# Attention scores of a decoder layer in two matmul passes in place of three, with doubled key parts

## The chip, the core and the metric

The kernel runs on one core of one Trainium2 chip. The metric is device time in microseconds (us) of one launch; less is better. The work of the core is shared by TensorE (PE, matmuls; its weight loads are listed apart as PEld), VectorE (DVE), ScalarE (ACT) and SyncE (SP), which here only issues DMAs. GpSimd does almost nothing.

## What is computed

A decoder layer for 512 positions of width 1024: half-step SwiGLU FFN, a mixing stage, and a second FFN, with RMS norms between. The mixing stage has two attentions over one shared projection: a stick-breaking one (8 heads of 64) and a dilated sliding-window one (4 key/value heads of 64, three query groups each). The part around the change, cut from the reference:

```python
z = jnp.einsum('bhqd,bhkd->bhqk', qb, kb).astype(jnp.float32) * scale       # stick-breaking, 8 heads
...
sc = jnp.einsum('bhqd,bhqmd->bhqm', qblk[g], kg).astype(jnp.float32) * scale  # dilated, 3 groups x 4 heads
```

All of it is float32. The kernel gets that precision from TensorE by splitting each operand into a high part (the value rounded to the type `float32r`) and a low part (the rest), and adding three passes: high by high, high by low, low by high.

## The kernel before, in words

**Products.** `product` (lines 1176 to 1179) issues the three passes: line 1177 multiplies the high parts, 1178 takes the low part of the moving operand, 1179 the low part of the stationary one. Every projection "unit" (128 output columns over all 1024 inputs, `unit`, line 1206) is 8 such products of 128x512, so 24 matmuls; "Ua" and "Ub" are its first and second half.

**Order of the mixing stage.** `mix_schedule` (line 106) writes out one list of steps, and all engines walk through it in that order. There are 22 attention units (`MIX_ORDER`: q and k and v of four stick-breaking head pairs, and rq, rk, rv of two dilated pairs), then 8 gate units. Half units are used as filling between the attention steps: `scores` h is the score matmuls of stick-breaking head h, `suffix` h and `pv` h its later matmuls, `dscores` (j, r) the scores of dilated head j and residue r (16 of them), `dturn` transposes their probabilities and `dpv` multiplies them with the values.

**Query and key parts.** A unit of q or k holds a pair of heads: head 0 in rows 0 to 63, head 1 in rows 64 to 127. Step `fin` splits it: ACT copies the whole 128x512 tile into the high part (line 666, tiles `sq_hi`, `sk_hi`, `dq_hi`, `dk_hi`), DVE subtracts to make the low part (line 1029 or 1045). The rotary units (rq, rk) are first put together from four 32-row copies on ACT (line 632) and three DVE operations (971, 1035, 1040).

**Score matmuls.** Head a of a pair uses rows 64a to 64a+63 of all four tiles, so each pass works on 64 rows. Stick-breaking: four key blocks with 384 and 128 columns (bank 0), 256 (bank 1) and 512 (bank 2), three passes each, and a bf16 mask matmul of 128 rows for each block (line 1364). Dilated: three groups with 512, 128 and 128 columns, three passes each, then two mask matmuls (lines 1408 and 1409). Lines 1349 and 1398 make PE wait until the low parts of the pair exist.

**Weights.** SP loads one 512 KB unit of weights at a time into a ring of four (`load`, line 417, DMA at line 423). The load of unit u waits until DVE has made the low part of unit u-4 (`w_lo`, line 762), because that frees the ring slot.

## Time and profile before

| | us |
|---|---|
| median of 3 runs (1153.1 to 1154.5) | 1153.97 |
| the profiled execution's own time | 1153.61 |
| its span, first to last instruction | 1151.8 |
| PE busy | 1113.0 (97%) |
| DVE busy | 774.1 (67%) |
| ACT busy | 543.4 (47%) |
| mean granted TensorE clock, 1 is 2.4 GHz | 0.982 |

How to read it: a matmul's start is when its first column goes in; matmuls overlap, so what a matmul costs is the distance from its start to the start of the next one, not its own duration. In the chain of work that ended last PE has 84%, DVE 9%, ACT 4%. The mixing stage runs from about 375 to 660 us.

### The profile page before, as it was taken

How to read it: one execution, taken by the hardware profiler on the slowest of the kernel's cores; microseconds unless marked ns; L12 is line 12 of the kernel's file. 1: busy time of each engine (PE TensorE's matmuls, PEld its weight loads, DVE VectorE, ACT ScalarE, POOL GpSimd, SP SyncE). 2: the span in 40 equal slices, each digit the busy share in tenths (PEclk: the TensorE clock that was granted, in tenths of full speed). 3: DMA queues.
4: the chain of work that ended last, by engine and by line, in shares of the span. 5: the costliest groups of instructions: out<-in, count | busy, mean ns of one | idle time of the engine just before them, and what ended most of it. 6: DMA issues, size and time to landing. Idle time of an engine off the chain costs nothing.

```text
span 1151.8 us, 15666 instructions
## 1 busy us (share of the span) xinstructions
PE 1113.0 (97%) x6058; PEld 953.9 (83%) x6066; DVE 774.1 (67%) x1085; ACT 543.4 (47%) x874; POOL 0.2 (0%) x4
## 2 busy tenths in 40 slices
PE   7799999999999999998899999999899999999996
PEld 6689899988998788887677788888798899989985
DVE  6866378845878778677575555666785478637854
ACT  6544155523653456666555433323553256424641
POOL 0000000000000000000000000000000000000000
PEclk9999999999999999998899999999999999999998
DMA  8133233332324212111020123433233232333221
GB/s 283 56 110 92 92 111 107 98 108 92 99 72 123 84 44 66 46 55 41 33 73 28 38 87 94 140 105 95 74 104 99 92 111 96 98 100 110 80 68 74
DMA packets 32904, 102.99 MB, mean 89 GB/s; under 512 B 4160, under 2 KB 5568, under 8 KB 32832
## 3 DMA queue, kind: packets, MB, share of 16 engines
q1 hardware_dynamic: 32832, 102.01, 28.1%
q8 instruction: 47, 0.77, 0.3%
q14 instruction: 25, 0.20, 0.1%
HBM read 99.90 MB, written 2.10 MB: 89 GB/s over the span
## 4 chain that ended last, share of the span: by engine, by line
PE 84%; DVE 9%; ACT 4%; issue 3%; DMA 0%; DVEq 0%; SPq 0%; ACTq 0%
PE acc_pair L1177 24%; PE acc_pair L1179 23%; PE acc_pair L1178 23%; PE pair_bank L1177 2%; PE pair_bank L1178 2%; PE pair_bank L1179 2%; DVE w_lo L762 2%; PE bank L1177 1%; PE bank L1179 1%; PE bank L1178 1%; ACT w_hi L474 1%; ACT rope L632 1%; DVE t_lo L815 1%; PE bank L1185 1%; DVE rstd L787 1%
## 5 line engine op out<-in xcount | busy, mean ns | idle before, releaser
L1177 PE MATMUL acc_pair<-xg_hi,w_hi 128*128 128x512 f32 (+1 forms) x684 | 265.7, 388 | 7.2 <-DVE w_lo L992 7.2
L1178 PE MATMUL acc_pair<-xg_lo,w_hi 128*128 128x512 f32 (+1 forms) x684 | 259.8, 380 | 0.0
L1179 PE MATMUL acc_pair<-xg_hi,w_lo 128*128 128x512 f32 (+1 forms) x684 | 258.6, 378 | 0.0
L474 ACT ACTIVATE w_hi<-w_raw 128x1024 fp32r<-128x1024 f32 (+2 forms) x158 | 152.6, 975 | 152.0 <-PE acc_pair L1179 151.9
L762 DVE TENSOR_TENSOR w_lo<-w_raw,w_hi 128x1024 fp32r<-128x1024 f32 (+2 forms) x158 | 177.5, 1125 | 47.2 <-ACT w_hi L474 46.5
L1177 PEld LDWEIGHTS acc_pair<-xg_hi,w_hi 128*128 128x128 f32 x684 | 131.9, 193 | 29.9 <-issue 8.4
L1179 PEld LDWEIGHTS acc_pair<-xg_hi,w_lo 128*128 128x128 f32 x684 | 131.2, 192 | 25.0
L1178 PEld LDWEIGHTS acc_pair<-xg_lo,w_hi 128*128 128x128 f32 x684 | 132.1, 193 | 20.2 <-issue 0.7
L1179 PE MATMUL acc_pair<-hid_hi,w_lo 128*128 128x512 f32 x352 | 138.8, 394 | 0.0
L1178 PE MATMUL acc_pair<-hid_lo,w_hi 128*128 128x512 f32 x352 | 138.2, 393 | 0.0
L1177 PE MATMUL acc_pair<-hid_hi,w_hi 128*128 128x512 f32 x352 | 136.9, 389 | 0.0
L931 DVE SCALAR_TENSOR_TENSOR x<-acc_pair,x 128x512 f32<-128x512 f32 x56 | 38.7, 692 | 114.0 <-PE acc_pair L1179 113.8
L1178 PEld LDWEIGHTS acc_pair<-hid_lo,w_hi 128*128 128x128 f32 x352 | 66.1, 188 | 15.1
L1177 PEld LDWEIGHTS acc_pair<-hid_hi,w_hi 128*128 128x128 f32 x352 | 66.1, 188 | 14.4
L1179 PEld LDWEIGHTS acc_pair<-hid_hi,w_lo 128*128 128x128 f32 x352 | 66.2, 188 | 13.4
L510 ACT ACTIVATE s_hi<-s_raw 128x1536 fp32r<-128x1536 f32 x36 | 53.5, 1487 | 48.2 <-DVE s_raw L835 48.2
L850 DVE TENSOR_TENSOR s_lo<-s_raw,s_hi 128x1536 fp32r<-128x1536 f32 x36 | 63.3, 1759 | 13.9 <-ACT s_hi L510 13.9
L1177 PE MATMUL acc_pair<-t_hi,s_hi 128*128 128x256 f32 x216 | 61.1, 283 | 2.6 <-ACT acc_pair L559 2.6
L862 DVE TENSOR_TENSOR acc_pair<-acc_pair,ysum 128x512 f32<-128x512 f32 x36 | 25.2, 700 | 57.2 <-PE acc_pair L1179 57.2
L1179 PE MATMUL acc_pair<-t_hi,s_lo 128*128 128x256 f32 x216 | 61.1, 283 | 0.0
L1178 PE MATMUL acc_pair<-t_lo,s_hi 128*128 128x256 f32 x216 | 61.0, 282 | 0.0
L525 ACT ACTIVATE gate<-gate 128x512 f32<-128x512 f32 x44 | 27.5, 626 | 48.1 <-DVE gate L864 48.1
(217 smaller groups left out, 2092.8 us busy)
## 6 DMA issues: line engine op xcount, KB each, us to landing
w_raw<-in_w13b SPq DMA_DIRECT2D x44, 512.0 KB, 3.6
w_raw<-in_w13a SPq DMA_DIRECT2D x40, 512.0 KB, 3.6
w_raw<-in_wmix SPq DMA_DIRECT2D x22, 512.0 KB, 3.5
w_raw<-in_w2a SPq DMA_DIRECT2D x16, 512.0 KB, 3.6
w_raw<-in_w2b SPq DMA_DIRECT2D x16, 512.0 KB, 3.6
w_raw<-in_wgate SPq DMA_DIRECT2D x8, 512.0 KB, 3.5
w_raw<-in_wend SPq DMA_DIRECT2D x8, 512.0 KB, 3.5
w_raw<-in_wo SPq DMA_DIRECT2D x8, 512.0 KB, 3.6
```

Source lines behind the costliest of these rows:

```text
L474: act.activation(w_hi[:, s, 0:width], w_raw[:, s, 0:width], ACT.Copy).then_inc(whi_done, 1)
L510: act.activation(s_hi[:, g % 2], s_raw[:], ACT.Copy).then_inc(s_hi_done, 1)
L525: act.activation(gate[:, f % 2, :], gate[:, f % 2, :], ACT.Silu).then_inc(silu_done, 1)
L632: act.activation(rope2[to:to + HD // 2, t % 2, :].rearrange("c (r p) -> c r p", r=DIL), acc[w % RING][c:c + HD // 2, :].rearrange("c (p r) ...
L762: dve.tensor_tensor(w_lo[:, s, 0:width], w_raw[:, s, 0:width], w_hi[:, s, 0:width].bitcast(F32), ALU.subtract).then_inc(wlo_done, 1)
L787: dve.reciprocal(rstd[:], mean[:]).then_inc(rstd_done, 1)
L850: dve.tensor_tensor(s_lo[:, g % 2], s_raw[:], s_hi[:, g % 2].bitcast(F32), ALU.subtract).then_inc(s_lo_done, 1)
L862: dve.tensor_tensor(late, late, p5, ALU.add).then_inc(p5_added, 1)
L931: dve.scalar_tensor_tensor(x[:, m, :], acc[s][:], scale, x[:, m, :], ALU.mult, ALU.add).then_inc(acc_read[s], 1)
L1177: pe.matmul(o, w_h, r_h, start=first, stop=False, skip_group_check=check)
L1178: pe.matmul(o, w_h, r_l, start=False, stop=False, skip_group_check=check)
L1179: return pe.matmul(o, w_l, r_h, start=False, stop=last, skip_group_check=check)
```

## The change

The tiles of query and key parts are laid out anew. Each head gets its own slot of 128 rows: in `sq2` and `dq2` the high part of the query lies in the head's 64 rows and the low part in the other 64 rows. In `sk2` and `dk2` the high part of the key lies in the head's 64 rows, and a DMA copies it into the other 64 rows (two DMAs of 64x512 float32, 128 KB each, per key unit; six key units). One pass of 128 rows then gives key high by query high plus key high by query low; a second pass of 64 rows gives key low by query high. For this

- each score product is 2 matmuls: one of 128 rows, one of 64 rows (before: 3 of 64 rows);
- ACT makes the high part in two instructions of 64x512 (before: one of 128x512), for each of the 16 q, k, rq and rk units; DVE makes the low part in two as well;
- SP issues the two copies of key unit w right behind the weight load of unit w+7, after a wait for the high parts (`op_hi_done`);
- PE waits for the copies (`twin_done`) ahead of the scores that use them.

The core of the diff (the renaming of buffers, and the counts `split_parts` in other waits, are left out):

```diff
@@ sync engine @@
-            for u in range(MIX, GATE):
-                load(u, 0, A["wmix"][u - MIX])
-            for u in range(GATE, END):
-                load(u, 0, A["wgate"][u - GATE])
+            for u in range(MIX, END):
+                load(u, 0, A["wmix"][u - MIX] if u < GATE else A["wgate"][u - GATE])
+                if u - 7 in KEYS:
+                    sp.wait_ge(op_hi_done, split_parts(u - 7 - MIX + 1))
+                    for head in (0, 1):
+                        key = stacked(u - 7, head)
+                        sp.dma_start(key[head_rows(head + 1), :].bitcast(F32), key[head_rows(head), :].bitcast(F32)).then_inc(twin_done, 16)
@@ scalar engine, fin @@
-                    act.activation(dst, src, ACT.Copy).then_inc(op_hi_done, 1)
+                    if what in ("v", "rv"):
+                        act.activation(dst, src, ACT.Copy).then_inc(op_hi_done, 1)
+                    else:
+                        for head in (0, 1):
+                            rows = head_rows(head)
+                            act.activation(stacked(w, head)[rows, :], src[rows, :], ACT.Copy).then_inc(op_hi_done, 1)
@@ vector engine, fin (q and k; rq and rk alike) @@
-                        dve.wait_ge(op_hi_done, fin)
-                        dve.tensor_tensor(lo[:, pair % 2, :], src, hi[:, pair % 2, :].bitcast(F32),
-                                          ALU.subtract).then_inc(op_lo_done, 1)
+                        dve.wait_ge(op_hi_done, split_parts(fin))
+                        for head in (0, 1):
+                            rows, hi = head_rows(head), stacked(w, head)
+                            lo = hi[head_rows(head + 1), :] if what == "q" else sk_lo[rows, pair % 2, :]
+                            dve.tensor_tensor(lo, src[rows, :], hi[rows, :].bitcast(F32),
+                                              ALU.subtract).then_inc(op_lo_done, 1)
@@ tensor engine, scores @@
-                    pe.wait_ge(op_lo_done, through(("q", hp, 0), ("k", hp, 0)))
+                    pe.wait_ge(op_lo_done, split_parts(through(("q", hp, 0), ("k", hp, 0))))
+                    pe.wait_ge(twin_done, 32 * (KEYS.index(MIX + MIX_ORDER.index(("k", hp, 0))) + 1))
...
-                            product(o, sk_hi[rows, hp % 2, ks], sk_lo[rows, hp % 2, ks],
-                                    sq_hi[rows, hp % 2, P * i:SEQ], sq_lo[rows, hp % 2, P * i:SEQ],
-                                    n == 0, False, True)
+                            pe.matmul(o, sk2[:, hp % 2, a, ks], sq2[:, hp % 2, a, P * i:SEQ], start=n == 0,
+                                      stop=False, skip_group_check=True)
+                            pe.matmul(o, sk_lo[rows, hp % 2, ks], sq2[rows, hp % 2, a, P * i:SEQ], start=False,
+                                      stop=False, skip_group_check=True)
@@ tensor engine, dscores @@
-                    product(bank[0], dq_hi[jp][rows, 0, own], dq_lo[jp][rows, 0, own], dk_hi[jp][rows, :],
-                            dk_lo[jp][rows, :], True, False, True)
-                    for g in (1, 2):
-                        product(bank[1][:, (g - 1) * P:g * P], dq_hi[jp][rows, g, own], dq_lo[jp][rows, g, own],
-                                dk_hi[jp][rows, own], dk_lo[jp][rows, own], g == 1, False, True)
+                    for g in range(NG):
+                        o = bank[1][:, (g - 1) * P:g * P] if g else bank[0]
+                        keys = own if g else slice(0, SEQ)
+                        pe.matmul(o, dq2[jp][:, a, g, own], dk2[jp][:, a, keys], start=g < 2, stop=False,
+                                  skip_group_check=True)
+                        pe.matmul(o, dq2[jp][rows, a, g, own], dk_lo[jp][rows, keys], start=False, stop=False,
+                                  skip_group_check=True)
```

PE, the first scores of the mixing stage (head 0 of the first pair), before. The names are output, moving and stationary operand; the last number is the columns:

```order
L1177 MATMUL pair_bank<-sq_hi,sk_hi 128x384 [waits consts_made,const_loaded,mean_done,op_lo_done]
L1178 MATMUL pair_bank<-sq_lo,sk_hi 128x384
L1179 MATMUL pair_bank<-sq_hi,sk_lo 128x384
L1177 MATMUL pair_bank<-sq_hi,sk_hi 128x128
L1178 MATMUL pair_bank<-sq_lo,sk_hi 128x128
L1179 MATMUL pair_bank<-sq_hi,sk_lo 128x128
L1364 MATMUL pair_bank<-mask_sb,identb 128x128 x2
L1177 MATMUL pair_bank<-sq_hi,sk_hi 128x256
L1178 MATMUL pair_bank<-sq_lo,sk_hi 128x256
L1179 MATMUL pair_bank<-sq_hi,sk_lo 128x256
```

And with the change (`sq` and `sk` are `sq2` and `sk2`):

```order
L1386 MATMUL pair_bank<-sq,sk 128x384 [waits consts_made,mean_done,const_loaded,twin_done,op_lo_done]
L1388 MATMUL pair_bank<-sq,sk_lo 128x384
L1386 MATMUL pair_bank<-sq,sk 128x128
L1388 MATMUL pair_bank<-sq,sk_lo 128x128
L1391 MATMUL pair_bank<-mask_sb,identb 128x128 x2
L1386 MATMUL pair_bank<-sq,sk 128x256
L1388 MATMUL pair_bank<-sq,sk_lo 128x256
L1391 MATMUL pair_bank<-mask_sb,identb 128x128
L1386 MATMUL bank<-sq,sk 128x512
```

Each block has one matmul less, and the wait at the head of the scores has `twin_done` in addition. A matmul of line 1386 works on 128 rows, one of line 1388 on 64.

SP, the loads of the mixing units before, all in one run:

```order
L423 DMA w_raw<-in_w2a 128x768 [waits wlo_done] x4
L423 DMA w_raw<-in_wmix 128x1024 [waits wlo_done] x22
L423 DMA w_raw<-in_wgate 128x1024 [waits wlo_done] x8
```

And with the change:

```order
L438 DMA w_raw<-in_wmix 128x1024 [waits wlo_done] x9
L471 DMA sk<-sk 64x512 [waits op_hi_done]
L471 DMA sk<-sk 64x512
L438 DMA w_raw<-in_wmix 128x1024 [waits wlo_done] x3
L471 DMA sk<-sk 64x512 [waits op_hi_done]
L471 DMA sk<-sk 64x512
L438 DMA w_raw<-in_wmix 128x1024 [waits wlo_done] x2
L471 DMA dk_0<-dk_0 64x512 [waits op_hi_done]
L471 DMA dk_0<-dk_0 64x512
```

The copies of the first key unit (number 1) stand behind nine weight loads, those of the second (number 4) three loads later, and so on; all go through the queue of the loads.

## Rows read from the trace of the kernel before

**Rows 1.** Windows; columns: us, busy PE PEld DVE ACT POOL, clock, DMA share, GB/s
```profile
375.00:521.00 146.00, 145.12 (x720) 117.60 (x718) 108.61 (x176) 87.77 (x149) 0.00 (x0) 0.98 0.18 58
521.00:620.00 99.00, 89.42 (x426) 70.12 (x432) 64.31 (x123) 58.45 (x95) 0.00 (x0) 0.93 0.16 48
```

**Rows 2.** Waits of PE, 375 to 660 us: total us, times, longest
```profile
PE pair_bank L1177 <- ACT prob L713: 3.9, 4, 2.3
PE bank L1418 <- ACT prob L719: 3.9, 4, 1.6
```

**Rows 3.** Timeline of PE, scores of head 1: start us, us, engine, line, operation
```profile
406.54 0.39 PE L1179 MATMUL acc_pair<-xg_hi,w_lo 128*128 128x512 f32 x1
406.86 0.44 PE L1177 MATMUL pair_bank<-sq_hi,sk_hi 64*128 64x384 f32 x1
407.13 0.33 PE L1178 MATMUL pair_bank<-sq_lo,sk_hi 64*128 64x384 f32 x1
407.31 0.33 PE L1179 MATMUL pair_bank<-sq_hi,sk_lo 64*128 64x384 f32 x1
```

**Rows 4.** Timeline of PE, one dilated score block
```profile
645.27 0.49 PE L1177 MATMUL pair_bank<-dk_hi,dq_hi 64*128 64x512 f32 x1
645.61 0.39 PE L1178 MATMUL pair_bank<-dk_lo,dq_hi 64*128 64x512 f32 x1
645.84 0.39 PE L1179 MATMUL pair_bank<-dk_hi,dq_lo 64*128 64x512 f32 x1
...
646.47 0.27 PE L1178 MATMUL pair_bank<-dk_lo,dq_hi 64*128 64x128 f32 x1
646.58 0.27 PE L1179 MATMUL pair_bank<-dk_hi,dq_lo 64*128 64x128 f32 x1
646.79 0.39 PE L1408 MATMUL pair_bank<-mask_g,identb 128*128 128x512 bf16 x1
```

**Rows 5.** Timeline of SP: when the weight loads w+7 of key units w went out
```profile
387.42 0.33 SPq L423 DMA_DIRECT2D w_raw<-in_wmix  x1
416.47 0.33 SPq L423 DMA_DIRECT2D w_raw<-in_wmix  x1
451.74 0.33 SPq L423 DMA_DIRECT2D w_raw<-in_wmix  x1
496.39 0.33 SPq L423 DMA_DIRECT2D w_raw<-in_wmix  x1
```

**Rows 6.** DMA issues: count, KB each, median us from issue to landing
```profile
w_raw<-in_wmix SPq DMA_DIRECT2D x22, 512.0 KB, 3.5
x<-in_xT SPq DMA_DIRECT2D x8, 256.0 KB, 6.8
w_raw<-in_wend SPq DMA_DIRECT2D x8, 256.0 KB, 2.6
w_raw<-in_wend SPq DMA_DIRECT2D x8, 128.0 KB, 2.2
```

**Rows 7.** Timeline of PE: first matmul of scores 0, 2, 4 and 6
```profile
388.04 0.44 PE L1177 MATMUL pair_bank<-sq_hi,sk_hi 64*128 64x384 f32 x1 [0.71 <-DVE sk_lo L1029]
419.57 0.44 PE L1177 MATMUL pair_bank<-sq_hi,sk_hi 64*128 64x384 f32 x1
459.10 0.44 PE L1177 MATMUL pair_bank<-sq_hi,sk_hi 64*128 64x384 f32 x1
499.41 0.44 PE L1177 MATMUL pair_bank<-sq_hi,sk_hi 64*128 64x384 f32 x1
```

**Rows 8.** Groups with shapes: a copy of 64 rows on ACT | busy us, mean ns
```profile
L699 ACT ACTIVATE ys_hi<-ysum 64x512 fp32r<-64x512 f32 x8 | 5.0, 628 | 0.3 <-DVE ysum L1081 0.2
```

**Rows 9.** Timeline around the split of dilated key unit 17
```profile
553.73 0.63 ACT L666 ACTIVATE dk_hi<-roped 128x512 fp32r<-128x512 f32 x1
554.47 0.69 DVE L1045 TENSOR_TENSOR dk_lo<-roped,dk_hi 128x512 fp32r<-128x512 f32 x1 [1.80 <-ACT dk_hi L666]
557.15 0.66 PE L1418 MATMUL bank<-identf,prob 128*128 128x128 f32 x4 [1.55 <-ACT prob L719]
```

**Rows 10.** Window behind the first scores: same columns as rows 1
```profile
390.00:395.00 5.00, 5.00 (x16) 3.71 (x16) 3.53 (x7) 4.84 (x9) 0.00 (x0) 0.66 0.04 16
```

More of the change, by code:

```diff
@@ L177, in through, with split_parts @@
     return max(MIX_ORDER.index(u) for u in units) + 1
+def split_parts(n):
+    return sum(1 if what in ("v", "rv") else 2 for what, _, _ in MIX_ORDER[:n])
+KEYS = [u for u in FINS if mix_kind(u)[0] in ("k", "rk")]
 ROPES = [u for u in FINS if mix_kind(u)[0] in ("rq", "rk")]
@@ L269, in build @@
                 prob = sb("prob", [P, 2, 6 * P], F32, att)
-                dq_hi = [None, None]
-                dq_lo, dk_hi, dk_lo, dv = ([None, None] for _ in range(4))
+                dq2, dk2, dk_lo, dv = ([None, None] for _ in range(4))
                 def dl_buffers(jp, where):
-                    dq_hi[jp] = sb(f"dq_hi{jp}", [P, NG, SEQ], F32R, where)
-                    dq_lo[jp] = sb(f"dq_lo{jp}", [P, NG, SEQ], F32R, where)
-                    dk_hi[jp] = sb(f"dk_hi{jp}", [P, SEQ], F32R, where)
+                    dq2[jp] = sb(f"dq2_{jp}", [P, 2, NG, SEQ], F32R, where)
+                    dk2[jp] = sb(f"dk2_{jp}", [P, 2, SEQ], F32R, where)
                     dk_lo[jp] = sb(f"dk_lo{jp}", [P, SEQ], F32R, where)
@@ L346, in build @@
         op_lo_done = sem("op_lo_done")
+        twin_done = sem("twin_done")
         z_done = sem("z_done")
@@ L381, in head_rows, with stacked @@
             return slice(HD * (h % 2), HD * (h % 2) + HD)
+        def stacked(w, head):
+            what, pair, g = mix_kind(w)
+            if what == "q":
+                return sq2[:, pair % 2, head, :]
+            if what == "k":
+                return sk2[:, pair % 2, head, :]
+            return dq2[pair][:, head, g, :] if what == "rq" else dk2[pair][:, head, :]
         def v_parts(t):
@@ L648, in _ @@
                         act.wait_ge(raw_done, n + 1)
-                        dst = (sq_hi if what == "q" else sk_hi)[:, pair % 2, :]
                         src = raw[:, w % 2, :]
@@ L652, in _ @@
                         act.wait_ge(rope_step, 2 * (ROPES.index(w) + 1))
-                        dst = dq_hi[pair][:, g, :] if what == "rq" else dk_hi[pair][:]
                         src = roped[:]
@@ L1040, in _ @@
                         dve.tensor_tensor(roped[:], src, turn, ALU.add).then_inc(rope_step, 1)
-                        hi = dq_hi[pair][:, g, :] if what == "rq" else dk_hi[pair][:]
-                        lo = dq_lo[pair][:, g, :] if what == "rq" else dk_lo[pair][:]
                         dve.wait_ge(rope_step, 2 * t + 2)
-                        dve.wait_ge(op_hi_done, fin)
-                        dve.tensor_tensor(lo, roped[:], hi.bitcast(F32), ALU.subtract).then_inc(op_lo_done, 1)
+                        dve.wait_ge(op_hi_done, split_parts(fin))
+                        for head in (0, 1):
+                            rows, hi = head_rows(head), stacked(w, head)
+                            lo = hi[head_rows(head + 1), :] if what == "rq" else dk_lo[pair][rows, :]
+                            dve.tensor_tensor(lo, roped[rows, :], hi[rows, :].bitcast(F32),
+                                              ALU.subtract).then_inc(op_lo_done, 1)
                     else:
                         hi, lo = v_parts(sv[:, pair % 2, :, :] if what == "v" else dv[pair][:])
-                        dve.wait_ge(op_hi_done, fin)
+                        dve.wait_ge(op_hi_done, split_parts(fin))
                         dve.tensor_tensor(lo,
@@ L1203, in bank_free @@
                 else:
-                    pe.wait_ge(op_lo_done, last - MIX + 1)
+                    pe.wait_ge(op_lo_done, split_parts(last - MIX + 1))
             def unit(u0, i, rhs, ks, before=None, half=None):
@@ L1382, in _ @@
                     hp = w // 2
-                    pe.wait_ge(op_lo_done, through(("v", hp, 0)))
+                    pe.wait_ge(op_lo_done, split_parts(through(("v", hp, 0))))
                     pe.wait_ge(a_split, 3 * w + 3)
@@ L1421, in _ @@
                     jp = w // 2
-                    pe.wait_ge(op_lo_done, through(("rv", jp, 0)))
+                    pe.wait_ge(op_lo_done, split_parts(through(("rv", jp, 0))))
                     pe.wait_ge(pt_split, DIL * (w + 1))
```

14 lines of the change are left out of this document (7 added, 7 removed).

## Prediction, made before the changed kernel was run

> **What bounds the kernel now.** The windows come first, since the change touches only the mixing stage. From 375 to 521 us PE is busy 145.1 of 146 us at a clock of 0.98; from 521 to 620 us it is busy 89.4 of 99 us at 0.93 [rows 1]. So the first part is bound by the matmuls, and the second (the dilated attention) by turns by the matmuls and by something that PE waits for. The list of waits names it: the probabilities, 3.9 us in four waits of the score matmuls and 3.9 us in four waits of the transposes [rows 2]. Behind both stands one chain: scores on PE, then maximum, exp, sum and scaling on DVE and ACT, then the transposes on PE. Whatever joins that chain on DVE or ACT is paid; whatever leaves PE there is paid back only in part. For the rest I read the timelines instruction by instruction, because the change takes matmuls that are short.
>
> **What the removed pass costs.** One pass of 384 columns takes 0.18 us from start to start [rows 3], one of 512 takes 0.23 and one of 128 takes 0.11 [rows 4]; for 256 columns I take 0.12, between them. A stick-breaking head has one block of each width, so it loses 0.18 + 0.11 + 0.12 + 0.23 = 0.64 us; eight heads lose 5.1 us. A dilated block loses 0.23 + 2 x 0.11 = 0.45 us; sixteen lose 7.2 us. Together 12.3 us, all on PE.
>
> **What the new passes add on PE.** Before, a block went through its passes with 64 rows throughout, and the number of rows changed only at its ends. What such a change costs can be read. Coming from 128 rows, the first score matmul starts 0.32 us after a 512-column pass that otherwise takes 0.23: 0.09 of nothing. It then takes 0.27 us to the next start, where the same pass takes 0.18 afterwards: another 0.09 to 0.11, in which its weights are loaded in the open [rows 3]. The dilated block shows the same, 0.34 against 0.23 for its first pass, and at its end, from 64 rows to 128, 0.21 against 0.11 [rows 4]. So a change of rows costs 0.09 us of drain and 0.11 of open loading, 0.20 in all; where the pass behind it has 128 columns the loading was what it cost before, so the pass goes from 0.11 to 0.25 (drain, load, 0.05 of columns): 0.14 more. The new code alternates 128 and 64 rows. The Trainium skill (TensorEngine Tiling (Array Packing), Key Properties) says that changing the tiling mode drains TensorE; by that rule, which gives no time, the trace agrees, with 0.09 us at each change.
>
> Counted out: a stick-breaking head before had three changes to 64 rows (at its start and behind two masks); now it has four, one per block, and one more back to 128 rows between the two blocks of bank 0. Two changes at 0.20 make +0.40, so a head comes to -0.64 + 0.40 = -0.24 and eight to **-1.9 us**. A dilated block now has a first pass of 0.23, a second of 0.41 (0.09 + 0.11 + 0.21) and four narrow ones of 0.25, then a drain of 0.09: 1.73 us. Before it was 1.52 from its first start to the mask [rows 4] plus the drain ahead, 1.61. That is +0.12 a block, **+1.9 us** for sixteen. On PE alone the change is worth nothing.
>
> **The copies.** They are new, and they are late by construction: those of key unit w leave behind the load of unit w+7, and this load leaves when DVE has the low part of w+3. The loads that matter went out at 387.42, 416.47, 451.74 and 496.39 us [rows 5]; the scores that need these keys began at 388.04, 419.57, 459.10 and 499.41 [rows 7]. A weight load lands 3.5 us after its issue; 128 KB alone lands after 2.2, and from 128 to 512 KB that is 0.43 us for each 128 KB [rows 6]. Do the copies queue behind the load? The same 256 KB take 2.6 us alone and 6.8 in the crowd at the start [rows 6], so transfers of this queue do stand behind each other. I take 3.5 + 2 x 0.43 = 4.4 us from the load's issue; the lower bound is 3.0 (issued 0.4 and 0.7 after the load, each landing as if alone), the upper 5.0. The skill (DMA: Bandwidth & Descriptors, Queues, rings and completion order) says each engine takes the descriptors of a ring in order; by that rule the copies come behind the load's data, and nothing here shows it for copies inside the chip.
>
> - Scores 0: the split halves (below) put the load at 388.0; + 4.4 is 392.4, against 388.04: **+4.4 us** (bounds 3.0 and 5.0). PE has nothing else in its queue: it is in order, and all units behind the scores wait too.
> - Scores 2: 416.5 + 4.4 = 420.9 against 419.6: **+1.4** (0 and 2).
> - Scores 4: 456.1 against 459.1: hidden, 3 us to spare.
> - Scores 6: 496.4 + 0.6 of a longer split + 4.4 = 501.4 against 499.4: **+2.0** (0.5 and 2.7).
> - The dilated keys are copied tens of us ahead: hidden. SP's own waits for the high parts hold the next load back by nothing, since that load waits for a DVE step that comes later in the list.
>
> **The halves.** A 64x512 copy on ACT takes 0.63 us [rows 8], as long as one of 128 rows [rows 9]; the same holds for DVE. Sixteen units so add 16 x 0.60 us to both, and since DVE waits for both halves, a split that lies on the chain grows by 1.2 us. In the stick-breaking part PE is ahead of nothing that this delays, except near 521 us, where DVE has no idle time left behind the last rq unit. In the dilated part the chain runs through the splits: DVE waits 1.80 us for `dk_hi`, makes `dk_lo`, and the transposes wait 1.55 us behind that [rows 9]. Four more splits lie there (rk, and three rq of pair 1). Five splits at 1.2 are 6.0; some 1.0 of it falls into gaps that PE fills with other matmuls: **+5.0 us** (bounds 1.5 and 8).
>
> **The clock.** After the short wait and the thin scores at 388 us the granted clock of a 5 us window is 0.66 [rows 10], so 3.4 us at the lower level (1.2 GHz), worth 1.7 us. A stop of 4.4 us in the same place, and two new ones, make one more such stretch likely: **+1.7** (bounds -1.7 and +5).
>
> **Sum.** 4.4 + 1.4 + 2.0 - 1.9 + 1.9 + 5.0 + 1.7 = +14.5 us. The profiled execution took 1153.61 us, so 1168.1; it lies 0.4 us under the median of the runs, so I say 1168.3. A measurement of this kernel can tell about 0.2% (2.3 us) from no change.
>
> **Rivals.**
> 1. *The drains are not paid* (faster). If the 64-row weights could be loaded under a running 128-row pass, PE gains the full 12.3 us; with halves wholly hidden and copies at the lower bounds (3.0 + 0 + 0.5) the sum is 12.3 - 3.5 = 8.8 less: 1145; with the copies as forecast 1149. The point from which it decides is a change of rows under 0.06 us. Against it: 0.09 and the open load at every change in rows 3 and 4. Chance 5%.
> 2. *The copies overtake the load.* Then they cost 3.0 + 0 + 0.5 in place of 7.8: 1164. For it: 128 KB alone lands in 2.2. Chance 22%.
> 3. *The halves are hidden.* DVE was busy only 64.3 of 99 us in the dilated part [rows 1]; if slack takes most of 5.0 the time is 1164, with rival 2 together 1160. Chance 18%.
> 4. *The chain of DVE and ACT takes over earlier.* DVE and ACT lie close behind PE from 465 us on; then splits of q and rq there count too (+3), and the clock falls at every stop (+3): 1175. Chance 15%.
> 5. *Nothing changes* because gains on PE and waits cancel, near 1154: 2%. That the passes do not go is excluded: PE has 80 matmuls less in the order, 4 for each of eight heads and 3 for each of sixteen blocks.
>
> **How the numbers follow.** The forecast has 38%. The range takes in rivals 2, 3 and 4 and stops short of the ends where all bounds meet: 1158 to 1176. Faster has rival 1 and a little for two favourable bounds together (6%), same 2%, slower the rest (92%).
>
> **What would show it.** PE: starts of a 128-row and the following 64-row score pass 0.09 us further apart than columns need, and each dilated block near 1.7 us. Waits: PE on the copies at scores 0, 2 and 6, about 5, 1.4 and 2 us. DMA issues: 128 KB copies landing about 4 us after issue. Dilated part: PE's waits for the probabilities grown from 7.8 to about 12 us. Wrong, if the first wait is under 2 us, if a block takes under 1.5 us, or if PE's waits for the probabilities stay near 8.

## The result, and the profile after

| | before | changed |
|---|---|---|
| median of the runs | 1154.01 us (1153.1 to 1154.5) | 1176.19 us (1173.58 to 1182.47) |
| ratio to before, 95% interval | | 1.0201, 1.016 to 1.0242 |
| profiled execution, its span | 1153.61, 1151.8 us | 1175.81, 1173.6 us |

The change is slower by 22.2 us, where 14.3 were forecast: the sign was right, and the time lies 0.2 us above the range. From the start to 375 us (PE busy 360.7 us before, 360.9 now) and over the last 491 us (478.1 and 478.2) the two traces differ by nothing that matters; all of it happens in the mixing stage. Its windows, in the columns of [rows 1], with the end of the stage added:

```profile
375.00:521.00 146.00, 133.61 (x597) 104.04 (x595) 103.35 (x164) 82.47 (x138) 0.00 (x0) 0.91 0.21 63
521.00:620.00 99.00, 89.23 (x391) 66.42 (x391) 67.63 (x123) 61.54 (x103) 0.00 (x0) 0.93 0.14 41
620.00:700.00 80.00, 79.02 (x355) 59.96 (x354) 43.56 (x80) 39.36 (x61) 0.00 (x0) 1.00 0.17 49
```

Up to 521 us PE was busy 145.12 us before and is busy 133.61 now, and the clock of that stretch fell from 0.98 to 0.91. The waits of PE, 375 to 725 us, answer to [rows 2]:

```profile
PE pair_bank L1386 <- issue: 10.9, 3, 6.3
PE bank L1449 <- ACT prob L740: 5.4, 3, 2.9
PE pair_bank L1435 <- ACT prob L734: 3.8, 4, 2.1
PE bank L1210 <- DVE dq L1069: 1.6, 1, 1.6
PE bank L1210 <- issue: 1.5, 2, 1.0
```

The first line is the wait of the scores for the copied rows: its releaser is called "issue" because the profile ties no engine to it, and a DMA had to land. The two waits for the probabilities grew only from 7.8 to 9.2 us. The first scores, and the copies that they wait for, against [rows 5] and [rows 7]:

```profile
388.60 0.33 SPq L438 DMA_DIRECT2D w_raw<-in_wmix  x1
388.97 1.17 SPq L471 DMA_DIRECT2D sk<-sk  x2
...
393.87 0.66 PE L1386 MATMUL pair_bank<-sq,sk 128*128 128x384 f32 x1 [6.28 <-issue]
```

The load went out 1.2 us later than before, and PE could go on 5.3 us after it. By the DMA issues a copy lands after 4.2 us (median) where it stands behind a load, and after 2.3 for the dilated keys:

```profile
sk<-sk SPq DMA_DIRECT2D x8, 128.0 KB, 4.2
...
dk<-dk SPq DMA_DIRECT2D x4, 128.0 KB, 2.3
```

The clock behind that stop and behind two later ones (windows of 5 us, columns as in [rows 10]):

```profile
390.00:395.00 5.00, 1.13 (x2) 0.57 (x2) 0.88 (x2) 0.00 (x0) 0.00 (x0) 0.64 0.48 143
395.00:400.00 5.00, 5.00 (x15) 3.08 (x15) 1.67 (x3) 3.54 (x8) 0.00 (x0) 0.50 0.00 0
400.00:405.00 5.00, 5.00 (x22) 4.06 (x21) 4.71 (x9) 3.66 (x5) 0.00 (x0) 0.84 0.00 0
430.00:435.00 5.00, 5.00 (x14) 2.85 (x14) 0.69 (x1) 3.39 (x7) 0.00 (x0) 0.50 0.00 2
580.00:585.00 5.00, 5.00 (x14) 3.70 (x14) 2.70 (x7) 1.71 (x3) 0.00 (x0) 0.50 0.32 105
```

At 0.50 (1.2 GHz) PE is busy all the time, and a projection pass of 512 columns starts every 0.43 us in place of every 0.23. The same place cost before one window of 0.66 [rows 10]. But a stretch at the lower clock also comes without a stop. The kernel before has windows of 0.82 and 0.84 from 480 to 490 us, and between 390 and 510 us its PE stands still nowhere for more than 0.15 us at a time. Its window from 485 us:

```profile
485.00:490.00 5.00, 5.00 (x20) 4.00 (x20) 3.12 (x6) 4.29 (x9) 0.00 (x0) 0.84 0.00 0
```

A dilated block and the scores of head 1, which answer to [rows 4] and [rows 3]:

```profile
645.35 0.39 PE L1435 MATMUL pair_bank<-dk,dq 128*128 128x512 f32 x1
645.67 0.50 PE L1437 MATMUL pair_bank<-dk_lo,dq 64*128 64x512 f32 x1
646.10 0.33 PE L1435 MATMUL pair_bank<-dk,dq 128*128 128x128 f32 x1
646.35 0.32 PE L1437 MATMUL pair_bank<-dk_lo,dq 64*128 64x128 f32 x1
646.60 0.33 PE L1435 MATMUL pair_bank<-dk,dq 128*128 128x128 f32 x1
646.86 0.32 PE L1437 MATMUL pair_bank<-dk_lo,dq 64*128 64x128 f32 x1
647.12 0.39 PE L1439 MATMUL pair_bank<-mask_g,identb 128*128 128x512 bf16 x1
```

```profile
414.24 0.33 PE L1386 MATMUL pair_bank<-sq,sk 128*128 128x384 f32 x1
414.50 0.44 PE L1388 MATMUL pair_bank<-sq,sk_lo 64*128 64x384 f32 x1
414.87 0.33 PE L1386 MATMUL pair_bank<-sq,sk 128*128 128x128 f32 x1
```

The block takes 1.77 us (645.35 to 647.12) where 1.73 was forecast, with starts 0.25 apart for narrow passes, and 384 columns take 0.26 and 0.37 to the next start where they took 0.18.

**A ledger.** To compare kernels I count three things between 375 and 725 us: the waits of PE (the list above, summed), the time that the lower clock takes ((1 - granted clock) x 25 us, summed over fourteen windows of 25 us), and the rest of the difference of the spans, which is work of PE. All are against the kernel before, which has 10.8 us of waits and 10.5 us of clock. Where the passes are unchanged the rest should be 0 and comes out between -3.8 and +2.1, so it is good to some 3 us. Spans and ledger are of the one profiled execution, which can lie off the median: by 3.6 us below it for e9, 2.7 below for e2, 2.4 above for e11.

| kernel | median us | span | waits | clock | rest |
|---|---|---|---|---|---|
| changed | 1176.19 | +21.8 | +12.4 | +10.3 | -0.9 |
| e1 copies first | 1172.12 | +17.0 | +11.2 | +7.0 | -1.2 |
| e2 halves alone | 1169.71 | +13.4 | +9.8 | +5.0 | -1.4 |
| e3 copies alone | 1162.36 | +9.4 | +10.0 | +3.2 | -3.8 |
| e4 rows grouped | 1169.98 | +15.1 | +20.9 | +8.5 | -14.3 |
| e7 halves, q and k only | 1159.76 | +5.1 | +4.9 | +1.5 | -1.3 |
| e8 halves, rq and rk only | 1159.77 | +5.8 | +8.1 | +0.0 | -2.3 |
| e9 changed, old passes | 1175.57 | +18.4 | +13.5 | +7.0 | -2.1 |
| e10 doubled by GpSimd | 1175.31 | +21.3 | +10.2 | +12.0 | -0.9 |
| e11 low keys padded | 1161.67 | +10.2 | +24.8 | +6.5 | -21.1 |
| e12 both | 1158.93 | +7.3 | +22.3 | +5.2 | -20.2 |
| e13 fill, on before | 1148.48 | -5.4 | -1.4 | -5.3 | +1.3 |
| e14 fill, on e2 | 1165.44 | +12.0 | +7.4 | +3.5 | +1.1 |
| e16 e13, one step early | 1154.21 | +1.4 | +3.1 | -3.8 | +2.1 |
| e17 e14, one step early | 1169.04 | +14.3 | +8.7 | +6.8 | -1.2 |

So in the changed kernel the new passes are worth nothing, more than half of the loss is waiting, and nearly half is the lower clock. The two don't go in step: e8 has 8.1 us more of waits and no more of the lower clock, e3 10.0 and 3.2, e10 10.2 and 12.0.

### The profile page after: what moved, and what is told of

Same layout as the page of the kernel before. It is cut to its first block, busy times and chain, and to the rows that moved or that the text cites. A ratio compares the mean times of both kernels' runs of the same rounds, so it can differ in the third digit from the quotient of the medians.

```text
span 1173.6 us, 15558 instructions
## 1 busy us (share of the span) xinstructions
PE 1122.9 (96%) x5986; PEld 950.5 (81%) x5986; DVE 785.9 (67%) x1101; ACT 554.2 (47%) x890; POOL 0.2 (0%) x4
## 4 chain that ended last, share of the span: by engine, by line
PE 87%; DVE 6%; ACT 3%; issue 2%; DMA 0%; DVEq 0%; SPq 0%; ACTq 0%
PE acc_pair L1202 24%; PE acc_pair L1203 24%; PE acc_pair L1204 24%; PE pair_bank L1202 1%; PE pair_bank L1203 1%; PE pair_bank L1204 1%; PE bank L1202 1%; PE bank L1204 1%; PE bank L1203 1%; DVE w_lo L783 1%; PE bank L1210 1%; ACT w_hi L492 1%; PE bank L1212 1%; PE pair_bank L1437 1%; PE pair_bank L1388 1%
## 5 line engine op out<-in xcount | busy, mean ns | idle before, releaser
L1203 PEld LDWEIGHTS acc_pair<-hid_lo,w_hi 128*128 128x128 f32 x352 | 66.1, 188 | 15.1
L1204 PEld LDWEIGHTS acc_pair<-hid_hi,w_lo 128*128 128x128 f32 x352 | 66.2, 188 | 13.4
```

Source lines behind the costliest of these rows:

```text
L1203: pe.matmul(o, w_h, r_l, start=False, stop=False, skip_group_check=check)
L1204: return pe.matmul(o, w_l, r_h, start=False, stop=last, skip_group_check=check)
```

## The experiments

The runs came in five batches. The medians of the kernel before in them were 1152.9 to 1153.6 us; differences below are to the median of the same batch, and ratios carry their 95% interval. A few executions of the kernel before take 1146 to 1150 us, and the ratios, which aren't those of the medians, come out higher for it: e3 has 1.0121, where its medians give 1.0082. So a difference is good to some 2 to 6 us, as the interval beside it says.

**Batch 1: the parts of the change, one at a time.** e1 is the changed kernel with the two copies issued ahead of the load and not behind it:

```diff
-                load(u, 0, A["wmix"][u - MIX] if u < GATE else A["wgate"][u - GATE])
                 if u - 7 in KEYS:
...
                         sp.dma_start(key[head_rows(head + 1), :].bitcast(F32), key[head_rows(head), :].bitcast(F32)).then_inc(twin_done, 16)
+                load(u, 0, A["wmix"][u - MIX] if u < GATE else A["wgate"][u - GATE])
```

> The changed kernel with one thing moved: SP sends the two copies of a key unit ahead of the weight load of seven units later, no longer behind it. Theory A (copies queue behind the 512 KB load, and the waits and the slow clock behind them are the larger part of the loss): a copy lands about 2.3 us after its issue in place of 4.2; PE stands still 6.3 - 2 = 4.3 us at scores 0 and 0 to 1 us at scores 2 and 6, in place of 10.9 us in all; fewer us at the lower clock level; time 1176 - 6 to 9 = 1167 to 1170. Rival (the copies are slow whatever is ahead, as moves between partitions): landing stays near 4 us, time within 2 us of 1176.

Measured: 1172.12 us, 1.0187 (1.0147 to 1.0227). A copy now lands 2.3 us after its issue and not 4.2, so it did stand behind the load:

```profile
sk<-sk SPq DMA_DIRECT2D x8, 128.0 KB, 2.3
```

But only 4 us of the time go, less than theory A's 6 to 9 and more than the rival's 2, and the intervals of the two kernels overlap. PE's waits for the copies fall from 10.9 to 7.4 us: 4.2 at the first scores, none at scores 2, and 3.2 at scores 6, where 0 to 1 was expected.

e2 is the kernel before in which only the splits are cut, both on ScalarE and on VectorE (the VectorE part for `sq_lo`, `sk_lo` is the same edit):

```diff
-                    act.activation(dst, src, ACT.Copy).then_inc(op_hi_done, 1)
+                    act.activation(dst[0:HD, :], src[0:HD, :], ACT.Copy)
+                    act.activation(dst[HD:P, :], src[HD:P, :], ACT.Copy).then_inc(op_hi_done, 1)
...
-                        dve.tensor_tensor(lo, roped[:], hi.bitcast(F32), ALU.subtract).then_inc(op_lo_done, 1)
+                        dve.tensor_tensor(lo[0:HD, :], roped[0:HD, :], hi[0:HD, :].bitcast(F32), ALU.subtract)
+                        dve.tensor_tensor(lo[HD:P, :], roped[HD:P, :], hi[HD:P, :].bitcast(F32), ALU.subtract).then_inc(op_lo_done, 1)
```

> The kernel before, with only the splits of q, k, rq and rk made in two instructions of 64 rows on ACT and two on DVE; matmuls, copies and waits are as before. Theory H (my term of +5.0): PE's waits for the probabilities grow from 7.8 to about 12, time 1157.5 to 1160. Rival (slack takes them): within 1.5 us of 1154.

Measured: 1169.71 us, 1.0167 (1.0127 to 1.0207), so +16.7 us for an edit that computes the same and was priced at 5.0; theory H's 1157.5 to 1160 and its rival are both far off. PE's waits in it:

```profile
PE bank L1425 <- ACT prob L723: 6.4, 4, 3.0
PE pair_bank L1184 <- ACT prob L717: 3.9, 4, 2.3
PE pair_bank L1184 <- DVE sk_lo L1035: 2.7, 2, 2.5
PE bank L1192 <- DVE sv L1056: 1.8, 1, 1.8
PE bank L1192 <- DVE dq_lo L1052: 1.7, 1, 1.7
```

Against [rows 2] only 2.5 us are new waits for the probabilities; the others lie at the first scores, and at the products with the values, stops for which the forecast had no price for the halves.

e3 is the kernel before with the copies alone, into a spare tile that nothing reads, and with PE's waits for them:

```diff
+                    for head in (0, 1):
+                        sp.dma_start(spare[head_rows(head + 1), n % 2, head, :], key[head_rows(head), :].bitcast(F32)).then_inc(twin_done, 16)
...
+                    pe.wait_ge(twin_done, 32 * (KEYS.index(MIX + MIX_ORDER.index(("k", hp, 0))) + 1))
```

> The kernel before, with only the copies added (same place in SP's queue, same size, from the whole high part of the key into a spare tile that nobody reads) and PE's waits for them. If the waits with the clock behind them are the larger part of the loss: PE stands still about 5, 1.5 and 2 us at scores 0, 2 and 6 and the time is 1154 + 9 of waiting + 4 to 6 of half clock = 1167 to 1169. Rival (stops cost their own length only, the clock comes from the new passes): 1161 to 1163, with the us at the lower level as before the change, about 20.

Measured: 1162.36 us, 1.0121 (1.0065 to 1.0177), so +9.4 us by the medians (7.5 to 20.4 by the interval), where 7.8 were forecast for the copies. The median lies in the rival's 1161 to 1163, and the lower clock took only 3.2 us more; but the rival's reason, that the clock comes from the new passes, doesn't hold, since e9 below has the old ones and 7.0 us more. The waits behind the copies (5.1, 2.4 and 4.2 us at scores 0, 2 and 6):

```profile
PE pair_bank L1189 <- issue: 11.8, 3, 5.1
```

e4 is the changed kernel with the passes of 128 rows of a bank (of a block) first and those of 64 rows after them, so that the rows change once and not at each pass:

```diff
                             pe.matmul(o, sk2[:, hp % 2, a, ks], sq2[:, hp % 2, a, P * i:SEQ], start=n == 0,
                                       stop=False, skip_group_check=True)
+                        for i, col in parts:
+                            o = bank[b][:, col:col + SEQ - P * i]
+                            ks = slice(P * i, P * i + P)
                             pe.matmul(o, sk_lo[rows, hp % 2, ks], sq2[rows, hp % 2, a, P * i:SEQ], start=False,
```

> The changed kernel with the passes of 128 rows of a bank (stick-breaking) or a block (dilated) first and those of 64 rows behind them: two changes of rows less in each of eight heads, four less in each of sixteen blocks. Theory D (a change costs 0.20 us, 0.14 before a narrow pass): a dilated block takes 1.2 us in place of 1.77, a head 0.3 less; 8.8 + 2.4 = 11 us less PE time, of which the dilated stage hands on what it is not waiting for: time 1166 to 1170. Rival (changes of rows are cheap, the rest is waiting): within 2 us of 1176.

Measured: 1169.98 us, 1.0175 (1.0133 to 1.0216), in theory D's range; a dilated block takes 1.18 us, where 1.2 was expected. By the ledger it freed 13 us of PE's work and got back 6 of time: the waits grew by 8.5 us over those of the changed kernel.

**Batch 2: where the halves cost.** Four kernels, each the kernel before with a part of the edit of e2: ScalarE's halves only; VectorE's only; both for q and k only (the condition `what in ("q", "k")` ahead of the halves); both for rq and rk only.

> The kernel before, with ScalarE's splits of the query and key units as two instructions of 64 rows, VectorE's subtractions whole. Theory A (every split stands in a row raw, high, low, and the units that a step of the program needs follow it closely, so each added instruction on either engine reaches TensorE): ScalarE's half costs about half of the 16.7 us of both, 7 to 9 us, 1160 to 1162. Theory B (ScalarE has room, VectorE, busier, is the one that passes it on): 2 us at most, 1155. Theory C (the loss is mostly the clock that falls at some stop of TensorE and a stop comes or doesn't): no sum, one of the two has nearly all of it.

> The kernel before, with VectorE's subtractions of the query and key units as two instructions of 64 rows, ScalarE's splits whole. Theory A: the other half of the 16.7 us, 7 to 9 us, 1160 to 1162, so that the two add up. Theory B: nearly all of it, 1167 to 1169. Theory C: no sum.

> The kernel before, with halves on both engines for the units of the stick-breaking heads alone (q, k: 8 splits). The record counted halves only from about 521 us on, so of the splits ahead of that nothing: by that 1154. Theory A (all splits count): 8 of 16 splits, and they stand where VectorE is busiest: 7 to 10 us, 1160 to 1163, seen in waits for sk_lo at the scores of the heads.

> The kernel before, with halves on both engines for the units of the dilated heads alone (rq, rk: 8 splits, of which most are done in the stretch where TensorE waits for the probabilities). By the record all of the +5.0 us: 1159. Theory A: 7 to 9 us, 1160 to 1162, with waits for the probabilities over the 7.8 us of the kernel before by 2 to 4 us and a wait for dq_lo.

| | median us | difference | ratio |
|---|---|---|---|
| e5 ScalarE only | 1157.92 | +4.3 | 1.0041 (1.0025 to 1.0057) |
| e6 VectorE only | 1160.99 | +7.4 | 1.0062 (1.0046 to 1.0079) |
| e7 q and k only | 1159.76 | +6.2 | 1.0059 (1.0042 to 1.0075) |
| e8 rq and rk only | 1159.77 | +6.2 | 1.0055 (1.0039 to 1.0072) |

No place and no engine has the cost alone, which is nearest to theory A, though e5, e7 and e8 lie under its ranges, the parts sum to 11.7 and 12.4, and both together cost 16.7. B falls, and so does C's form in which one part has nearly all; that the parts give no clean sum stays. e8 is near the 1159 that the forecast's term gives for the dilated part. The forecast's sentence that in the stick-breaking part PE is ahead of nothing that the halves delay is wrong by the 6.2 us of e7, whose timeline shows one of its places, the first scores, with a wait that was 0.71 us [rows 7]:

```profile
388.81 0.44 PE L1183 MATMUL pair_bank<-sq_hi,sk_hi 64*128 64x384 f32 x1 [2.50 <-DVE sk_lo L1035]
```

**Batch 3: passes, row changes, and who makes the doubled rows.** e9 has e2's halves and e3's copies and keeps the three passes. e10 is the changed kernel with GpSimd in place of the DMAs:

```diff
+        @block.gpsimd
+        def _(pool):
+            for u in KEYS:
+                pool.wait_ge(op_hi_done, split_parts(u - MIX + 1))
+                for head in (0, 1):
+                    key = stacked(u, head)
+                    pool.tensor_copy(key[head_rows(head + 1), :], key[head_rows(head), :].bitcast(F32)).then_inc(twin_done, 16)
```

e11 is the changed kernel with low keys in tiles of 128 rows, half of them zeros that GpSimd writes once, so that all passes have 128 rows; e12 is both.

```diff
-                            pe.matmul(o, sk_lo[rows, hp % 2, ks], sq2[rows, hp % 2, a, P * i:SEQ], start=False,
+                            pe.matmul(o, sk_lo[:, hp % 2, a, ks], sq2[:, hp % 2, a, P * i:SEQ], start=False,
```

> The kernel before with all that the change adds around the passes (halves on both engines, and the copies with TensorE's waits for them), but with its own three passes a product. The difference to the changed kernel is the price of the new passes alone, which the record puts at nothing (-1.9 for the stick-breaking heads, +1.9 for the dilated blocks). Theory A (halves 16.7 and copies 9.4 stand in different waits and add): 1178 to 1181, and then the new passes gained 2 to 4 us. Theory B (they share waits, since a copy can't begin before the halves are done and a stop hides the other's): 1168 to 1173, and then the new passes cost 3 to 8 us. In between, 1174 to 1177: they are worth nothing, as on record.

Measured: 1175.57 us, 1.0224 (1.018 to 1.0267), between theories A and B: what the change adds around the passes costs all of the loss, and the passes themselves nothing that can be measured (to some 5 us, the width of the intervals). Halves and copies are 16.7 and 9.4 alone and 22.7 together; whether they overlap at all isn't shown, since the gap of 3.4 lies within the noise.

> The changed kernel with the doubled rows of the keys written by GpSimd (8 + 4 copies of 64 rows) in place of SyncE's DMAs. Theory 1 (the price of the copies is the DMA's time and its place behind a 512 KB load): the wait of 6.3 us at the first scores falls to 3 us or less, those of 2.1 and 2.6 go: 1167 to 1170. Theory 2 (the price is that the twin is made behind the split at all; GpSimd is as slow as a DMA, or slows VectorE beside it): no change, 1174 to 1178.

Measured: 1175.31 us, 1.0213 (1.0174 to 1.0252): no gain, as theory 2 had it. GpSimd takes 1.04 us for 64 rows. The wait of 2.09 us at scores 2 goes. At the first scores PE now stops for `sk_lo` and for GpSimd, which end 0.5 us apart, and VectorE's two halves beside GpSimd took 1.70 us and not 1.40:

```profile
388.71 1.70 DVE L1056 TENSOR_TENSOR sk_lo<-raw,sk 64x512 fp32r<-64x512 f32 x2 [0.21 <-ACT sk L691]
...
388.82 2.07 POOL L486 CAST sk<-sk 64x512 fp32r<-64x512 f32 x2 [388.37 <-ACT sk L691]
...
390.99 0.62 PE L1390 MATMUL pair_bank<-sq,sk 128*128 128x384 f32 x1 [3.47 <-DVE sk_lo L1056]
```

At scores 6 the wait stays at 2.57 us, as long as for the DMAs:

```profile
509.94 0.41 PE L1390 MATMUL pair_bank<-sq,sk 128*128 128x384 f32 x1 [2.57 <-POOL sk L486]
```

PE is there at 507.4 us; ScalarE ends the high part at 507.6, VectorE the low part at 509.4 and GpSimd the copies at 509.8. So with no copy at all PE would have waited 2.0 us here for the two halves. In the changed kernel it came to this place 1.0 us after VectorE had ended (515.9 and 514.9 us): what PE saves at the earlier scores it meets again here, at the split. In e1 it comes 1.7 us ahead of VectorE's end.

The first scores come 2.9 us earlier than in the changed kernel, and the ledger has 2.2 us less of waits, but 1.7 more of clock.

> The changed kernel with the low parts of the keys in tiles of 128 rows whose other 64 rows are zeros (cleared once by GpSimd), so that every pass has 128 rows and TensorE never changes its rows inside a bank. Theory 1 (a change of rows costs 0.09 + 0.11 us, as on record: 9 changes a stick-breaking head with 8 heads, 5 a dilated block with 16): the blocks fall from 1.77 to about 1.3 us and the scores of a head from 2.77 to about 2.2, some 12 us of TensorE's time; in the stick-breaking heads 3 to 5 of them reach the time, in the dilated blocks they turn in part into waits for the probabilities: 1168 to 1172. Theory 2 (TensorE's time there is worth nothing, its waits grow by all of it): 1175 to 1177. Its output is the reference's.

Measured: 1161.67 us, 1.0087 (1.0058 to 1.0115), 14.5 us under the changed kernel, beyond both theories, which had at best 1168. The same kind of block as above has 128 rows all the way, and takes 0.94 us and not 1.77 (about 1.3 was expected):

```profile
640.57 0.48 PE L1452 MATMUL pair_bank<-dk,dq 128*128 128x512 f32 x1
640.88 0.40 PE L1454 MATMUL pair_bank<-dk_lo,dq 128*128 128x512 f32 x1
641.11 0.22 PE L1452 MATMUL pair_bank<-dk,dq 128*128 128x128 f32 x1
641.17 0.27 PE L1454 MATMUL pair_bank<-dk_lo,dq 128*128 128x128 f32 x1
641.28 0.28 PE L1452 MATMUL pair_bank<-dk,dq 128*128 128x128 f32 x1
641.39 0.28 PE L1454 MATMUL pair_bank<-dk_lo,dq 128*128 128x128 f32 x1
641.51 0.39 PE L1456 MATMUL pair_bank<-mask_g,identb 128*128 128x512 bf16 x1
```

The scores of a head take 1.58 us in place of 2.77. Eight heads and sixteen blocks make 22.8 us, and the ledger puts the row changes at 20 us of PE's work (-21.1 against -0.9), of which 12.4 come back as waits. Against the kernel before it is the whole 21.1: the padding removes also the row changes that the three passes of 64 rows had at each end of a block.

> Both of the last two edits in one kernel: doubled rows by GpSimd and low keys of 128 rows. If the two add: 1160 to 1164, so still slower than the kernel before by the halves that are left. If a shorter wait for the copy only uncovers the wait for the halves: 1165 to 1170. To beat the kernel before it would have to be under 1152, which no theory expects.

Measured: 1158.93 us, 1.0068 (1.0046 to 1.009), just under the 1160 to 1164 of adding: the best form of the two passes so far, and still slower than the three.

**Batches 4 and 5: by what mechanism the halves cost.** e13, e14 and e15 put another order of the fill on the kernel before, on e2 and on e12:

```diff
-DL_FILL = (1, 1, 1, 1, 1, 1, 2, 3, 1, 1, 1, 2, 1, 2, 2, 2)
+DL_FILL = (2, 1, 2, 1, 1, 1, 2, 2, 1, 1, 1, 2, 1, 2, 1, 2)
-SB_FILL = ((3, 1), (1, 1), (4, 1),
+SB_FILL = ((3, 1), (1, 1), (3, 1),
...
-    fill(4)
+    fill(5)
     s.append(("scores", 0))
```

> The kernel before with another order of its fill (half units of weights): one half unit more ahead of the scores of heads 0 to 2 (one less behind those of head 2), one more in the dilated blocks 0 and 2, one less in blocks 7 and 14. It is the control for the next two. Its waits on VectorE and for the probabilities there are small (0.7 before the first scores, 2.3 and 1.6 in the blocks): 1149 to 1153 if only these go, over 1154 if the places that give up a half unit begin to wait.

> The kernel before with halves on both engines (1169.7, +16.7 us) and the new order of the fill. Theory L (the halves cost latency: each wait of TensorE has one half unit of 5 us as its only cover, and the halves use up what was left of it): the waits of 2.5 us for sk_lo, 2.3 and 3.0 us for the probabilities go with the clock stretches behind them, and the excess over the control falls from 16.7 to 9 or less: 1158 to 1162. Theory T (throughput: ScalarE and VectorE can't keep up in these stretches, whatever the order): a wait removed comes back at the next step, the excess over the control stays 14 or more: 1165 to 1169.

> The changed kernel with low keys of 128 rows, doubled rows by GpSimd (1158.9; 33 us of waits of TensorE in the stage, 11 in the kernel before) and the new order of the fill. Theory L: 3.5 us for sk_lo, 3.0 and 3.4 us for the probabilities go: 1146 to 1152, and then the two passes beat the three. Theory T: 1156 to 1159.

| | median us | ratio |
|---|---|---|
| e13 on before | 1148.48 | 0.9964 (0.995 to 0.9978) |
| e14 on e2 | 1165.44 | 1.0112 (1.0082 to 1.0143) |
| e15 on e12 | 1158.60 | 1.0047 (1.0031 to 1.0062) |

The halves cost 17.0 us over their control, as many as before: theory L falls. By the ledger it is half and half: 8.8 us of waits and 8.8 of the lower clock, of 17.4 by the spans. The control gained, and by the clock: with the wait of 0.71 us gone, the window behind the first scores stays at full speed, where [rows 10] has 0.66:

```profile
390.00:395.00 5.00, 5.00 (x26) 3.69 (x25) 3.00 (x7) 4.43 (x9) 0.00 (x0) 1.00 0.21 88
```

The kernel before comes near this time too in some executions (1148.4 and 1149.3 us of 17 in this batch, at a mean clock of 0.987 and 0.986 where most have 0.984); e13 took 1147.3 to 1149.4 in all ten.

But theory T as I put it, that ScalarE and VectorE are full, isn't what the trace of e14 shows: from 550 to 575 us VectorE is busy 14.2 us and ScalarE 15.8. Around a wait of 3.65 us for the scaled probabilities (PE at 560.01) both work in turns:

```profile
554.29 0.63 ACT L669 ACTIVATE dk_hi<-roped 64x512 fp32r<-64x512 f32 x1
554.93 0.63 ACT L670 ACTIVATE dk_hi<-roped 64x512 fp32r<-64x512 f32 x1
...
555.66 0.68 DVE L1051 TENSOR_TENSOR dk_lo<-roped,dk_hi 64x512 fp32r<-64x512 f32 x1 [2.44 <-ACT dk_hi L670]
556.36 0.69 DVE L1052 TENSOR_TENSOR dk_lo<-roped,dk_hi 64x512 fp32r<-64x512 f32 x1
...
558.60 0.60 DVE L1122 TENSOR_TENSOR prob<-prob 128x128 f32<-128x128 f32 x2
...
559.23 0.72 ACT L723 ACTIVATE prob<-prob,stats 128x512 f32<-128x512 f32 x1 [2.40 <-DVE prob L1122]
```

VectorE stands idle 2.44 us for `dk_hi`, ScalarE then 2.40 us for VectorE. In [rows 9] the first of these was 1.80. So here each half of a split is added to a row of steps that wait for each other; that this is how the halves cost everywhere is read from the trace, and no run isolates it. e16 to e18 take this at its word, and move the next block's sum over its groups (dadd) ahead of the fin on e13, e14 and e15:

```diff
             s.append((half, u))
+            s.extend(behind)
...
-        fill(1)
+        fill(1, [("dadd", b) for b in blocks[n + 1:n + 2]])
```

> The control (kernel before in the new order of the fill, 1148.5) with one more move: a dilated block's sum over its groups (dadd: reciprocal, two additions on VectorE, the scaling on ScalarE) stands ahead of the fin of the half unit before it and no longer behind it. Theory C (chain: neither ScalarE nor VectorE is full there, but the fin's row rope, high, low lies in front of dadd, so that its length reaches the transposes): the waits for the scaled probabilities, 5.2 us in 5, go: 1141 to 1145. Theory T (both engines are full): 1147 to 1150.

> The same move in the kernel with halves (1165.4 in the new order; its control cost 16.9 us less). Theory C: the halves in the dilated blocks (four splits, 1.3 us each on the chain) no longer lie in front of the transposes, whose waits of 8.9 us in 5 go; what is left of the halves is the part of the stick-breaking heads and the wait for dq_lo: 1151 to 1157, an excess over e16_early_control of 8 to 12. Theory T: 1163 to 1166, the excess stays at 16 to 17.

> The same move in the changed kernel with low keys of 128 rows, doubled rows by GpSimd and the new order of the fill (1158.6, 13.2 us of waits for the scaled probabilities). Theory C: 10 us or more of them go: 1145 to 1150. Theory T: 1156 to 1159.

| | median us | ratio |
|---|---|---|
| e16 on e13 | 1154.21 | 1.001 (0.9997 to 1.0023) |
| e17 on e14 | 1169.04 | 1.0151 (1.0129 to 1.0174) |
| e18 on e15 | 1162.87 | 1.0094 (1.0072 to 1.0116) |

All three lost 3.6 to 5.7 us and lie above the ranges of both theories, and the excess of the halves fell only from 17.0 to 14.8. The waits for the scaled probabilities are gone in e17, and a longer one stands at the score matmuls, in the list of waits (total, times, longest):

```profile
PE pair_bank L1186 <- ACT prob L719: 8.9, 5, 5.6
```

The timeline of VectorE and of PE around it:

```profile
570.95 0.68 DVE L1053 TENSOR_TENSOR dq_lo<-roped,dq_hi 64x512 fp32r<-64x512 f32 x1 [2.44 <-ACT dq_hi L672]
571.65 0.69 DVE L1054 TENSOR_TENSOR dq_lo<-roped,dq_hi 64x512 fp32r<-64x512 f32 x1
572.37 0.96 DVE L1109 TENSOR_REDUCE stats<-pair_bank 128x1 f32<-128x768 f32 x1
...
574.68 0.76 PE L1186 MATMUL pair_bank<-dk_hi,dq_hi 64*128 64x512 f32 x1 [5.64 <-ACT prob L719]
```

Now the maximum of a block (L1109) stands in VectorE's order behind the low part of a query, and the exp behind it. That wait comes with the move and not with the halves: the control e16 has it at 5.7 us too. So moving this one step doesn't help, since another step of the softmax then stands behind the row. Theory C's picture of the row is what these two places show, but its number is refuted. Of the 14.8 us left (12.9 by the spans), the ledger makes most the clock: e17 has 5.6 us more waits than e16 and 10.5 more of the lower clock, with a rest of -3.3. Whether an order that breaks the row itself (the maximum and the sum both ahead of the low part) would hide the halves wasn't tried and stays open.

## Why the prediction was off in size

The miss can be read in two ways. By cause (e3 and e9), the term for the halves failed: 13.2 us on top of the copies, where 5.0 were forecast. By form (the ledger), the term for the clock failed: 10.3 us, where 1.7 were forecast.

- **The removed pass and the row changes** (-1.9 and +1.9): right. The block took 1.77 us against 1.73, and the scores of a head went from 2.93 (drain ahead of them included) to 2.77 us, -0.16 against -0.24. The ledger has -0.9 for all of PE's work, and e9 against the changed kernel shows no difference. Rival 1 was far off; but e11 shows that PE's work could be had, by making the row changes unnecessary.
- **The copies** (+7.8): right in kind, a little small. They cost 9.4 alone, and 10.9 us of waits in the changed kernel where 0.7 stood in the same place. At the first scores it was +5.8 and not +4.4: the load left at 388.60, where the text took 388.0, and PE went on 5.3 us behind it and not 4.4. (In e3, without the halves, this wait grew by just the 4.4.) Scores 2 and 6 waited 2.09 and 2.57 us where 1.4 and 2.0 were forecast; scores 4 did not wait, as forecast. Rival 2 is excluded by 4.2 against 2.3 us to landing.
- **The halves** (+5.0, bounds 1.5 and 8): the step that failed. Alone they cost 16.7 us, and 13.2 on top of the copies (e9 against e3, by their medians; 9.0 by the profiled executions, of which 3.5 are waits and 3.8 the lower clock). For the dilated part, which the term was made for, the size was right: 6.2 us (e8). What failed is the reason by which nothing else was counted, that in the stick-breaking part PE is ahead of nothing that the halves delay: there e7 measured 6.2 us. Both parts together cost 4.3 more than their sum, and for that no run gives the reason. The rival that the halves are hidden fell.
- **The clock** (+1.7, bounds -1.7 and +5): the term of the sum that was sized worst. It took 10.3 us more, 8.6 above the term, which is more than the 7.9 us that the forecast missed. The text made one more stretch likely behind the first stop; there were stretches behind scores 0, behind scores 2, at 455, around 500, at 520 and 560 us and behind the wait at 577. That stops were followed by a lower clock was right, but they have no fixed price in it, and what decides whether such a stretch comes isn't shown: e8 added 8.1 us of waits and none of it, and the kernel before has one with no stop ahead of it.
- **The waits in all** came out as forecast, 12.4 us against 7.8 + 5.0 = 12.8, and that is luck in part: those at the first matmuls of scores 0, 2 and 6 grew by 10.2 us and all others by 2.2. The waits for the probabilities, forecast at about 12 us, stayed at 9.2. By the text's own sign that speaks for hidden halves. They were not hidden: by e9 and e3 their cost lies in other waits and in the clock.
- **Rival 4** (the chain takes over earlier, clock falls at every stop: 1175) came closest to what happened. It had the two things that failed, but both too small (+3 where e7 has 6.2, and +3 where 8.6 were missing), so that its time fits is luck in part; worked out from 1168.3 it is 1174.3.

One slip stands in the sum itself: 1168.1 and 0.4 more make 1168.5, and the text says 1168.3. It changes nothing above.

## What to carry to other kernels

Look at the granted clock behind each stop of TensorE before pricing it: in the changed kernel the lower clock took nearly as much as the waits, and in the kernel before a stop of 0.7 us had such a stretch behind it. But take the price as a range: against the kernel before, e8 has none of it and e10 has 1.2 times its added waits. An instruction cut into two halves of the rows is doubled, and where two engines hand a tile back and forth that can add to the chain, even though both are idle a third of the time (VectorE was busy 68% and ScalarE 62% of 521 to 620 us in the changed kernel). And before trading a pass for another shape, look at what the shape does at its borders: alternating 128 and 64 rows ate the pass that was saved, and zeros in the other 64 rows were the cheaper form. And a wait that is shortened can come back at the next one: in e10 the wait at scores 2 went, and at scores 6 PE was ahead of the split itself.

## What was unexpected of the hardware

- Row changes are dearer than the 0.09 us of their drains: a dilated block with six passes of alternating rows takes 1.77 us, the same six with 128 rows throughout 0.94, and with the rows changed once (e4) 1.18.
- A lower granted clock came without a stop of PE: 0.82 and 0.84 from 480 to 490 us in the kernel before.
- GpSimd copying 64 x 512 beside VectorE (1.04 us each) came with VectorE's two halves going from 1.40 to 1.70 us.
- An order of the fill that only removes the wait of 0.71 us in the kernel before, and shifts others, made that kernel faster by 0.36% (0.22 to 0.5), 5.3 us of it clock in the profiled execution. e13 is the fastest kernel of this study, and it has none of the change.
